# Expert loop: gate and up of an expert pair as one product of 512 columns in one PSUM bank

## The chip, the cores and the metric

The kernel runs on one core of a Trainium2 chip. The metric is the device time of one execution in microseconds (us). The kernel before took 1553.9 us (median of 3 runs, 1553.81 to 1555.06).

## What is computed

One step of a two-layer decoder over 264 tokens (256 of a prompt, 8 samples), all in fp32. Each layer has a mixer and then a mixture of experts; the change touches the experts alone. Of the reference, cut to that part:

```python
def moe(h, w_router, b_router, w_gate, w_up, w_down, ws_gate, ws_up, ws_down):
    x = h.reshape(-1, D)                                   # 264 tokens x 1024
    ...                                                    # sigmoid scores, best 4 of 8 groups, top 8 of 64 experts
    combine = ...                                          # (T, 64): a token's weight for an expert, or 0
    for gi in range(N_GROUPS):
        hg = jnp.einsum('td,edf->tef', x, w_gate[sl])      # 1024 -> 256 for each expert
        hu = jnp.einsum('td,edf->tef', x, w_up[sl])
        hw = jax.nn.silu(hg) * hu * combine[:, sl, None]
        routed = routed + jnp.einsum('tef,efd->td', hw, w_down[sl])
    shared = (jax.nn.silu(x @ ws_gate) * (x @ ws_up)) @ ws_down
    return (routed + shared).reshape(Bn, L, D)
```

## The kernel before

Engines and semaphores are programmed by hand: each engine has its own block with its instructions in order, and `wait_ge` on named semaphores ties them together. The order on an engine is the order in its block.

**Expert loop.** Experts go in pairs, 32 pairs a layer (`NPAIR`), two layers. Each pair has 128 slots of tokens, 64 for each of its two experts `e`. The loop body of `pe`, `act`, `dve` and `pool` is written out for four pairs (`EBODY`). A pair needs six weight blocks ("units") of 1 MiB: gate, up and down of two experts. They lie in a ring of 12 slots (`ring`, `ESLOTS`), so two pairs fit; SyncE (`expert_load`, line 516) refills a slot as soon as `unit_used` says that TensorE is through with it.

**TensorE for one pair, in order** (lines 1105 to 1156):
1. `product(0)`: gate. For each of 8 chunks `c` of the 1024 inputs and each `e`, a product of 256 columns; expert 0 writes partitions 0 to 63 and expert 1 partitions 64 to 127 of PSUM bank 0, columns 0 to 255. Stationary is the 128x64 block of tokens (`xgT`), moving are 256 columns of the ring.
2. `slots()`: three transposes that turn the slot choice of the pair after next into token rows (bank 4).
3. `product(1)`: up, the same into bank 1.
4. The combine: 8 products of 264 columns, one for each output chunk `c`, that spread the finished rows of the pair before (`gout_tiles`) back over the tokens. They use banks 5 to 7 in turn: chunk `c` waits until VectorE has added chunk `c - 3` to the sum (`cb_add`).
5. Two transposes of the hidden rows `ghid` (wait for `ghid` of this pair), into bank 0, columns 256 to 511.
6. `rows_in`: eight transposes of the next pair's gathered tokens.
7. The down product: 8 products of 512 columns into banks 2 and 3.

Every fp32 product is two LDWEIGHTS and two MATMUL instructions in the trace, every transpose one of each.

**ScalarE for one pair:** Silu of the gate (waits for two `unit_used`), copy of the turned slots (`slot_tokens`), copy of the turned hidden rows, two copies of turned tokens, one copy of half of the down result (`os_a`).

**VectorE for one pair** (lines 1903 to 1914): `choose` (L1868), `take_weights` (L1881, L1882), `take_slots` (L1873, L1876; waits for ScalarE's `slot_tokens`), then `ghid` = Silu x weight x up (L1910), then the eight additions `add_back` (L1887), then the copy of the other half of the down result (L1914).

**GpSimd** gathers the token rows of the pair after next by an indirect DMA (L654) as soon as `take_slots` has written their indices.

Of the kernel before, what the change touches and what calls it, by code (L numbers as in the profile page):

```python
# [17 lines left out]
ALU = mybir.AluOpType  # L18
ACT = mybir.ActivationFunctionType
AX = mybir.AxisListType  # L20

P = 128
# [39 lines left out]
EBODY = 4  # L62
NTURN = NPAIR // EBODY
PU = 6
RU = NPAIR * PU


SEL_R = NPAIR + 2
# [101 lines left out]
def build(nc, ins, outs):  # L170
# [12 lines left out]
    with ExitStack() as ctx:  # L183
# [275 lines left out]
        def eslot(j):  # L459

            return (j + PU) % ESLOTS
# [5 lines left out]
        def _(sp):  # L467
# [45 lines left out]

            def expert_load(l, pair2, j):

                sp.dma_start(ring[:, eslot(j), :], expert_src(l, pair2 + (j // PU * 2 + j % 2), j % PU // 2)).then_inc(eload[eslot(j)], 16)

            def experts(l, last):

                sp.wait_ge(S["htok_out"], 32 * (l + 1))  # L520
                for n, j in sorted((last - 1 - ((last - 1 - j) % MSLOTS), j) for j in range(MSLOTS)):
                    wait_used(n)
                    expert_load(l, 0, PU + j)
                sp.wait_ge(S["round_set"], l + 1)
                first = sp.value_load(nrounds[0:1, 0:1], min_val=1, max_val=MAXR) if l else 0
                end = sp.value_load(nrounds[0:1, l:l + 1], min_val=1, max_val=(l + 1) * MAXR)

                with sp.Fori(first, end) as r:
                    with sp.Fori(0, RU // ESLOTS - 1) as i:
                        for j in range(ESLOTS):  # L530
                            sp.wait_ge(S["unit_used"], r * RU + i * ESLOTS + (j + 1) + ONE)
                            expert_load(l, (i + 1) * 4, j)

                    with sp.If(r + 1 < end):
                        for j in range(ESLOTS):
                            sp.wait_ge(S["unit_used"], r * RU + (RU - ESLOTS) + (j + 1) + ONE)
                            expert_load(l, 0, j)

                if l == 0:
                    sp.wait_ge(S["unit_used"], end * RU + ONE)  # L540

# [149 lines left out]
        def _(pe):  # L691
# [330 lines left out]
            def moe(l):  # L1022
# [76 lines left out]
                with pe.Fori(first, end) as r:  # L1099
# [4 lines left out]
                    with pe.Fori(0, NTURN) as i:  # L1104
                        for b in range(EBODY):
                            done1 = r * NPAIR + i * EBODY + (b + 1)
                            nb = (b + 1) % 2
                            s0 = eslot((b % 2) * PU)

                            def arrived_units(kind):  # L1110
                                for e in range(2):
                                    pe.wait_ge(eload[s0 + 2 * kind + e], r * (RU // ESLOTS * 16) + i * 32 + 16 * (b // 2 + 1))

                            def product(kind):
                                arrived_units(kind)
                                for c in range(DT):
                                    for e in range(2):
                                        x = mm(psum[64 * e:64 * e + 64, kind, 0:DE], xgT[:, c, 64 * e:64 * e + 64],
                                               ring[:, s0 + 2 * kind + e, c * DE:(c + 1) * DE], c == 0, c == DT - 1)
                                        if c == DT - 1:  # L1120
                                            x.then_inc(S["unit_used"], 1)

                            pe.wait_ge(S["xt_sb"], r * XT_R + i * 8 + (2 * b + 2))
                            pe.wait_ge(S["gsil"], done1 - 1 + ONE)
                            product(0)

                            pe.wait_ge(S["sel"], r * SEL_R + i * EBODY + (b + 3))
                            slots()

                            pe.wait_ge(S["ghid"], done1 - 1 + ONE)  # L1130
                            product(1)

                            pe.wait_ge(S["os_a"], done1 - 1 + ONE)
                            pe.wait_ge(S["os_b"], done1 - 1 + ONE)
                            for c in range(DT):
                                pe.wait_ge(S["cb_add"], r * CB_R + i * 32 + (8 * b + max(c - 2, 0)) + BACK0)
                                mm(psum[:, back_bank(c), 0:T], gout_tiles[:, c], selT[(b + 3) % 4]).then_inc(S["cb_mm"], 1)

                            pe.wait_ge(S["ghid"], done1 + ONE)
                            for j in range(2):  # L1140
                                last = tr(psum[:, 0, (2 + j) * P:(3 + j) * P], ghid[:, j])
                            last.then_inc(S["ht_mm"], 1)

                            pe.wait_ge(S["gat_" + "ab"[nb]], r * GAT_R + i * 32 + 16 * ((b + 1) // 2 + 1))
                            pe.wait_ge(S["selT_sb"], r * SEL_R + i * EBODY + (b + 3))
                            rows_in(xg[nb], r * CB_R + i * 32 + (8 * b + 6) + BACK0)

                            pe.wait_ge(S["ht_sb"], done1 + ONE)
                            arrived_units(2)
                            for n in range(2):  # L1150
                                for j in range(2):
                                    for e in range(2):
                                        x = mm(psum[64 * e:64 * e + 64, 2 + n, :], ghT[:, j, 64 * e:64 * e + 64],
                                               ring[:, s0 + 4 + e, j * D + n * 512:j * D + n * 512 + 512], j == 0, j == 1)
                                        if n == 1 and j == 1:
                                            x.then_inc(S["unit_used"], 1)
# [105 lines left out]
        def _(act):  # L1262
# [111 lines left out]
            def moe(l):  # L1374
# [35 lines left out]
                with act.Fori(first, end) as r:  # L1410
                    act.wait_ge(S["unit_used"], r * RU + ONE)
                    rows_in(r * XT_R)
                    with act.Fori(0, NTURN) as i:
                        for b in range(EBODY):
                            done1 = r * NPAIR + i * EBODY + (b + 1)
                            used0 = r * RU + i * (EBODY * PU) + b * PU
# [5 lines left out]
                            act.wait_ge(S["ht_mm"], done1)  # L1422
                            act.wait_ge(S["unit_used"], used0 + 4 + ONE)
                            f(ghT, psum[:, 0, 2 * P:4 * P].rearrange("p (j s) -> p j s", j=2), ACT.Copy).then_inc(S["ht_sb"], 1)
                            rows_in(r * XT_R + i * 8 + (2 * b + 2))
                            act.wait_ge(S["unit_used"], used0 + 6 + ONE)
# [47 lines left out]
        def _(dve):  # L1474
# [331 lines left out]
            def moe(l):  # L1806
# [91 lines left out]
                with dve.Fori(first, end) as r:  # L1898
                    with dve.Fori(0, NTURN) as i:
                        for b in range(EBODY):  # L1900
                            done1 = r * NPAIR + i * EBODY + (b + 1)
                            used0 = r * RU + i * (EBODY * PU) + b * PU
                            choose(i * 8 + (2 * b + 4))
                            take_weights(b, i * 8 + 2 * b, r * XT_R + i * 8 + (2 * b + 2))
                            take_slots((b + 2) % 4, r * SEL_R + i * EBODY + (b + 3))

                            dve.wait_ge(S["gsil"], done1 + ONE)
                            dve.wait_ge(S["wt_set"], done1 + ONE)
                            dve.wait_ge(S["unit_used"], used0 + 4 + ONE)
                            V.scalar_tensor_tensor(ghid.rearrange("p j f -> p f j"), gsil.rearrange("p (f j) -> p f j", j=2), wt[:, b:b + 1], psum[:, 1, 0:DE].rearrange("p (f j) -> p f j", j=2), ALU.mult, ALU.mult).then_inc(S["ghid"], 1)  # L1910
                            dve.wait_ge(S["cb_add"], r * CB_R + i * 32 + 8 * b + BACK0)
                            add_back(r * CB_R + i * 32 + 8 * b)
                            dve.wait_ge(S["unit_used"], used0 + 6 + ONE)
# [91 lines left out]
```

## Time and profile before

| what | value |
|---|---|
| time, median of 3 runs | 1553.9 us |
| profiled execution: its span, first to last instruction | 1551.6 us |
| TensorE matmul (PE) busy | 1472.9 us, 95% |
| TensorE weight load (PEld) busy | 982.9 us, 63% |
| VectorE (DVE) busy | 626.2 us, 40% |
| ScalarE (ACT) busy | 299.1 us, 19% |
| DMA moved, over the span | 523.24 MB, mean 337 GB/s |
| TensorE's granted clock, mean | 0.974 of full |

The profile is of one execution. Busy shares are averages over stages with different limits; the two expert loops lie at about 328 to 835 us and 1018 to 1525 us. Matmuls are pipelined and their ends are modelled, so a busy PE is not PE at its peak. Where the timeline gives "x32" the row is a run of 32 instructions, its second number the time from the first's start to the last's end. What stands in brackets at a row's end is the engine's idle time before it and what ended it.

### The profile page before, as it was taken

How to read it: one execution, taken by the hardware profiler on the slowest of the kernel's cores; microseconds unless marked ns; L12 is line 12 of the kernel's file. 1: busy time of each engine (PE TensorE's matmuls, PEld its weight loads, DVE VectorE, ACT ScalarE, POOL GpSimd, SP SyncE). 2: the span in 40 equal slices, each digit the busy share in tenths (PEclk: the TensorE clock that was granted, in tenths of full speed). 3: DMA queues.
4: the chain of work that ended last, by engine and by line, in shares of the span. 5: the costliest groups of instructions: out<-in, count | busy, mean ns of one | idle time of the engine just before them, and what ended most of it. 6: DMA issues, size and time to landing. Idle time of an engine off the chain costs nothing. (4 is left out here: it accounts for less than half of the span.)

```text
span 1551.6 us, 29339 instructions
## 1 busy us (share of the span) xinstructions
PE 1472.9 (95%) x11071; PEld 982.9 (63%) x11071; DVE 626.2 (40%) x1628; ACT 299.1 (19%) x624; POOL 116.3 (7%) x122
## 2 busy tenths in 40 slices
PE   5999889989999999999998999799999999999996
PEld 2767777556666666666665688666666666666664
DVE  2038573723334343433335233733433334343434
ACT  0013112311111111111113221321111111111112
POOL 0000143000000000000000000100000000000000
PEclk8999798999999999999999999899999999999998
DMA  9996524779999999999993871389999999999971
GB/s 390 362 366 272 178 55 182 285 299 404 409 420 420 410 417 412 412 415 410 418 401 144 329 296 44 120 338 400 419 415 418 419 411 413 417 414 417 413 294 29
DMA packets 81361, 523.24 MB, mean 337 GB/s; under 512 B 14213, under 2 KB 14341, under 8 KB 21019
## 3 DMA queue, kind: packets, MB, share of 16 engines
q1 hardware_dynamic: 68587, 495.84, 78.6%
q0 software_dynamic: 12720, 26.63, 5.1%
q8 instruction: 40, 0.66, 0.2%
q14 instruction: 14, 0.11, 0.0%
HBM read 537.18 MB, written 4.74 MB: 349 GB/s over the span
## 5 line engine op out<-in xcount | busy, mean ns | idle before, releaser
L693 PE MATMUL psum<-ring,arena 128*64 128x256 f32 (+2 forms) x5552 | 706.7, 412 | 4.3 <-ACT arena L1264 2.3
L693 PEld LDWEIGHTS psum<-ring,arena 128*64 128x64 f32 (+1 forms) x5552 | 369.8, 139 | 297.8 <-issue 160.9
L1264 ACT ACTIVATE arena<-psum 128x256 f32<-128x256 f32 (+4 forms) x464 | 210.4, 489 | 1024.2 <-PE psum L693 529.0
L693 PE MATMUL psum<-arena 128*128 128x264 f32 (+2 forms) x1840 | 285.5, 324 | 4.1 <-DVE arena L1720 2.1
L693 PEld LDWEIGHTS psum<-arena 128*128 128x128 f32 (+1 forms) x1840 | 225.1, 171 | 62.7 <-issue 28.4
L1887 DVE TENSOR_TENSOR arena<-arena,psum 128x264 f32<-128x264 f32 x528 | 226.6, 429 | 9.3 <-PE psum L693 2.0
L693 PE MATMUL psum<-hT,ring 128*128 128x264 f32 x928 | 215.8, 390 | 6.2 <-DVE hT L1587 2.7
L693 PEld LDWEIGHTS psum<-hT,ring 128*128 128x128 f32 x928 | 176.4, 192 | 48.3 <-issue 19.9
L1914 DVE COPY arena<-psum 128x512 f32<-128x512 f32 x64 | 44.3, 692 | 274.1 <-PE psum L693 274.1
L654 POOL DMA_INDIRECT arena<-h_rows,slot_idx x68 | 67.6, 995 | 972.7 <-DVE slot_idx L1876 916.6
L696 PE MATMUL psum<-K,arena 128*128 128x128 f32 (+4 forms) x961 | 125.6, 270 | 7.3 <-DMA arena<-h_rows,slot_idx 5.4
L696 PEld LDWEIGHTS psum<-K,arena 128*128 128x128 f32 (+4 forms) x961 | 105.5, 139 | 42.2 <-issue 30.9
L1910 DVE SCALAR_TENSOR_TENSOR arena<-arena,psum 128x256 f32<-128x256 f32 x64 | 42.7, 667 | 163.9 <-PE psum L693 163.9
L1873 DVE CUSTOM_DVE_ANT_0 arena<-arena,K 128x264 f32<-128x264 f32 x68 | 29.4, 433 | 196.7 <-ACT arena L1264 196.7
L693 PE MATMUL psum<-arena,ring 64*64 64x64 f32 (+2 forms) x576 | 61.2, 293 | 10.4 <-issue 4.5
L693 PE MATMUL psum<-ring,cT 128*32 128x512 f32 x384 | 54.3, 683 | 14.8 <-DMA ring<-in_w_mod 14.8
L693 PEld LDWEIGHTS psum<-arena,ring 64*64 64x64 f32 (+1 forms) x576 | 52.1, 181 | 17.6 <-issue 8.3
L1868 DVE TENSOR_TENSOR arena<-K,arena 88x384 f32<-88x384 f32 x68 | 37.1, 545 | 10.7 <-ACT arena L1264 8.3
L693 PEld LDWEIGHTS psum<-ring,cT 128*32 128x32 f32 x384 | 10.9, 121 | 42.6 <-issue 30.6
L693 PE MATMUL psum<-arena,K 128*32 128x66 f32 (+2 forms) x348 | 27.6, 294 | 8.3 <-ACT arena L1264 8.2
L1264 ACT ACTIVATE ring<-psum 128x264 f32<-128x264 f32 (+3 forms) x24 | 13.2, 566 | 92.3 <-PE psum L693 80.8
L693 PEld LDWEIGHTS psum<-arena,K 128*32 128x32 f32 (+2 forms) x348 | 19.3, 141 | 17.1 <-ACT arena L1264 13.8
(210 smaller groups left out, 478.8 us busy)
## 6 DMA issues: line engine op xcount, KB each, us to landing
ring<-in_moe_w_gate SPq DMA_DIRECT2D x128, 1024.0 KB, 11.4
ring<-in_moe_w_up SPq DMA_DIRECT2D x128, 1024.0 KB, 12.6
ring<-in_moe_w_down SPq DMA_DIRECT2D x128, 1024.0 KB, 9.5
ring<-in_w_mod SPq DMA_DIRECT2D x48, 1024.0 KB, 9.0
ring<-in_ab_w_in SPq DMA_DIRECT2D x13, 1024.0 KB, 7.8
ring<-in_gm_w_in SPq DMA_DIRECT2D x8, 1024.0 KB, 8.6
ring<-in_ab_w_out SPq DMA_DIRECT2D x4, 1024.0 KB, 5.7
ring<-in_gm_w_out SPq DMA_DIRECT2D x4, 1024.0 KB, 6.9
```

The source lines that it names most:

```text
L654: pool.indirect_dma_start(xg[jj % 2], None, h_rows[l], bass.IndirectOffsetOnAxis(slot_idx[:, jj:jj + 1], 0), bounds_check=T - 1, oob_is_er ...
L693: return nc.tensor.matmul(out, lhsT, rhs, start=start, stop=stop)
L696: return nc.tensor.transpose(out, in_, ident[0:in_.shape[0], 0:in_.shape[0]])
L1264: return nc.scalar.activation(out, in_, func, **kw)
L1868: V.tensor_tensor(slotsel[0:TR], iota, over(p, CAP), ALU.is_equal).then_inc(S["sel"], 1)
L1873: V.tensor_tensor_reduce(sel_tok, selT[jj], K[:, C_IOTA:C_IOTA + T], 1.0, float(NO_ROW), ALU.mult, ALU.add, idxf[:, jj:jj + 1]).then_inc(S ...
L1887: V.tensor_tensor(yacc[:, c, :], yacc[:, c, :], psum[:, back_bank(c), 0:T], ALU.add).then_inc(S["cb_add"], 1)
L1910: V.scalar_tensor_tensor(ghid.rearrange("p j f -> p f j"), gsil.rearrange("p (f j) -> p f j", j=2), wt[:, b:b + 1], psum[:, 1, 0:DE].rearr ...
L1914: V.tensor_copy(gout_tiles[:, :, 64:128], psum[:, 3, :].rearrange("p (d c) -> p c d", c=DT)).then_inc(S["os_b"], 1)
```

## The change

Gate and up of an expert are one product: its moving operand is a pair of pieces of 256 columns from two neighbouring ring slots, its output the 512 columns of bank 0, gate in the first half and up in the second. `slots()` follows it. For this, the ring order of a pair's units becomes gate 0, up 0, gate 1, up 1, down 0, down 1 (`UNIT_OF`), `unit_used` counts four products of a pair instead of six (`USES`, `USED_AT`), and the hidden rows are turned into bank 1 instead of bank 0. SyncE, ScalarE and VectorE wait for other counts; the order of the work on ScalarE and VectorE is as before.

```diff
 PU = 6
-RU = NPAIR * PU
+UNIT_OF = ((0, 0), (0, 1), (1, 0), (1, 1), (0, 2), (1, 2))
+USED_AT = (1, 1, 2, 2, 3, 4)
+USES = 4
+RU = NPAIR * USES
...
-                            sp.wait_ge(S["unit_used"], r * RU + i * ESLOTS + (j + 1) + ONE)
+                            sp.wait_ge(S["unit_used"], r * RU + i * (2 * USES) + (j // PU * USES + USED_AT[j % PU]) + ONE)
                             expert_load(l, (i + 1) * 4, j)
...
                             pe.wait_ge(S["xt_sb"], r * XT_R + i * 8 + (2 * b + 2))
-                            pe.wait_ge(S["gsil"], done1 - 1 + ONE)
-                            product(0)
+                            pe.wait_ge(S["ghid"], done1 - 1 + ONE)
+                            for c in range(DT):
+                                for e in range(2):
+                                    if c == 0:
+                                        arrived_unit(2 * e)
+                                        arrived_unit(2 * e + 1)
+                                    x = mm(psum[64 * e:64 * e + 64, 0, :].rearrange("p (k f) -> p k f", k=2), xgT[:, c, 64 * e:64 * e + 64],
+                                           ring[:, s0 + 2 * e:s0 + 2 * e + 2, c * DE:(c + 1) * DE], c == 0, c == DT - 1)
+                                    if c == DT - 1:
+                                        x.then_inc(S["unit_used"], 1)
 
                             pe.wait_ge(S["sel"], r * SEL_R + i * EBODY + (b + 3))
                             slots()
 
-                            pe.wait_ge(S["ghid"], done1 - 1 + ONE)
-                            product(1)
-
                             pe.wait_ge(S["os_a"], done1 - 1 + ONE)
                             pe.wait_ge(S["os_b"], done1 - 1 + ONE)
                             for c in range(DT):
...
                             for j in range(2):
-                                last = tr(psum[:, 0, (2 + j) * P:(3 + j) * P], ghid[:, j])
+                                last = tr(psum[:, 1, j * P:(j + 1) * P], ghid[:, j])
...
                             dve.wait_ge(S["gsil"], done1 + ONE)
                             dve.wait_ge(S["wt_set"], done1 + ONE)
-                            dve.wait_ge(S["unit_used"], used0 + 4 + ONE)
-                            V.scalar_tensor_tensor(ghid..., psum[:, 1, 0:DE]..., ALU.mult, ALU.mult).then_inc(S["ghid"], 1)
+                            dve.wait_ge(S["unit_used"], used0 + 2 + ONE)
+                            V.scalar_tensor_tensor(ghid..., psum[:, 0, DE:2 * DE]..., ALU.mult, ALU.mult).then_inc(S["ghid"], 1)
                             dve.wait_ge(S["cb_add"], r * CB_R + i * 32 + 8 * b + BACK0)
                             add_back(r * CB_R + i * 32 + 8 * b)
```

## Rows read from the trace of the kernel before

**Rows 1.** Stretch of the loop: length; PE, PEld, DVE, ACT, POOL busy; PEclk, DMA share, GB/s.
```profile
400.00:500.00 100.00, 100.00 (x686) 63.09 (x682) 38.85 (x103) 16.24 (x36) 6.93 (x7) 1.00 1.01 418
```

**Rows 2.** Waits at 400 to 800 us: engine's, then SyncE's queue: us, times, longest.
```profile
DVE arena L1873 <- ACT arena L1264: 71.7, 25, 2.9
DVE arena L1910 <- PE psum L693: 66.6, 26, 2.6
...
SPq L516 <- PE psum L693: 319.4, 76, 7.5
```

**Rows 3.** Line 1914, 400 to 800 us: durations, first and last start.
```profile
L1914 DVE COPY arena<-psum x25: 690/692/692, 410.3 to 791.1; 128x512 f32<-128x512 f32 x25
```

**Rows 4.** Timeline of one pair, TensorE: start, us, instruction, count.
```profile
604.01 0.28 PEld L696 LDWEIGHTS psum<-K,arena 88*128 88x128 f32 x3 [0.39 <-issue]
604.39 3.67 PE L693 MATMUL psum<-ring,arena 128*64 128x256 f32 x32
608.00 3.41 PEld L693 LDWEIGHTS psum<-arena 128*128 128x128 f32 x16 [0.39 <-issue]
613.33 0.14 PEld L693 LDWEIGHTS psum<-ring,arena 128*64 128x64 f32 x2 [0.29 <-issue]
616.33 1.65 PEld L693 LDWEIGHTS psum<-ring,arena 128*64 128x64 f32 x16 [0.29 <-issue]
```

**Rows 5.** The same timeline, ScalarE and VectorE.
```profile
604.23 0.67 ACT L1264 ACTIVATE arena<-psum 128x256 f32<-128x256 f32 x2 [2.93 <-PE psum L693]
604.93 0.43 DVE L1873 CUSTOM_DVE_ANT_0 arena<-arena,K 128x264 f32<-128x264 f32 x1 [2.85 <-ACT arena L1264]
605.41 0.15 DVE L1876 CAST slot_idx<-arena 128x1 uint32<-128x1 f32 x1
606.41 0.99 POOL L654 DMA_INDIRECT arena<-h_rows,slot_idx  x1 [14.81 <-DVE slot_idx L1876]
608.14 0.67 DVE L1910 SCALAR_TENSOR_TENSOR arena<-arena,psum 128x256 f32<-128x256 f32 x1 [2.58 <-PE psum L693]
608.75 3.55 DVE L1887 TENSOR_TENSOR arena<-arena,psum 128x264 f32<-128x264 f32 x8
```

**Rows 6.** Timeline in short windows: weight loads and products of 256 columns, one by one.
```profile
604.45 0.14 PEld L693 LDWEIGHTS psum<-ring,arena 128*64 128x64 f32 x2
607.47 0.14 PEld L693 LDWEIGHTS psum<-ring,arena 128*64 128x64 f32 x2
607.68 0.39 PE L693 MATMUL psum<-ring,arena 128*64 128x256 f32 x2
```

**Rows 7.** The same, of the combine.
```profile
608.55 0.39 PE L693 MATMUL psum<-arena 128*128 128x264 f32 x1
609.44 0.39 PE L693 MATMUL psum<-arena 128*128 128x264 f32 x1
```

**Rows 8.** Timeline at the second loop's start.
```profile
1006.04 0.70 DVE L1893 TENSOR_TENSOR arena<-arena,psum 128x528 f32<-128x528 f32 x1 [1.47 <-PE psum L693]
1006.82 2.52 PEld L693 LDWEIGHTS psum<-arena,ring 128*128 128x128 f32 x12 [0.82 <-issue]
1007.13 0.15 DVE L1876 CAST slot_idx<-arena 128x1 uint32<-128x1 f32 x1
1007.21 0.55 DVE L1868 TENSOR_TENSOR arena<-K,arena 88x384 f32<-88x384 f32 x1
1018.00 3.67 PE L693 MATMUL psum<-ring,arena 128*64 128x256 f32 x32 [1.16 <-ACT arena L1264]
```

**Rows 9.** The page's DMA issues: count, KB each, us from issue to landing.
```profile
ring<-in_moe_w_up SPq DMA_DIRECT2D x128, 1024.0 KB, 12.6
```

**Rows 10.** A stretch that waits for weights, columns as in the first group.
```profile
10.00:20.00 10.00, 7.85 (x100) 2.67 (x96) 1.00 (x2) 0.32 (x1) 0.00 (x0) 1.00 1.01 424
```

**Rows 11.** Timeline at the first loop's start.
```profile
325.59 1.09 PE L696 MATMUL psum<-K,arena 128*128 128x128 f32 x8 [4.17 <-DMA arena<-h_rows,slot_idx]
327.84 6.46 PE L693 MATMUL psum<-ring,arena 128*64 128x256 f32 x32 [1.16 <-ACT arena L1264]
```

More of the change, by code:

```diff
@@ L514, in expert_load @@
             def expert_load(l, pair2, j):
-                sp.dma_start(ring[:, eslot(j), :], expert_src(l, pair2 + (j // PU * 2 + j % 2), j % PU // 2)).then_inc(eload[eslot(j)], 16)
+                sp.dma_start(ring[:, eslot(j), :], expert_src(l, pair2 + (j // PU * 2 + UNIT_OF[j % PU][0]), UNIT_OF[j % PU][1])).then_inc(eload[eslot(j)], 16)
             def experts(l, last):
@@ L528, in experts @@
                 with sp.Fori(first, end) as r:
-                    with sp.Fori(0, RU // ESLOTS - 1) as i:
+                    with sp.Fori(0, NPAIR * PU // ESLOTS - 1) as i:
                         for j in range(ESLOTS):
-                            sp.wait_ge(S["unit_used"], r * RU + i * ESLOTS + (j + 1) + ONE)
+                            sp.wait_ge(S["unit_used"], r * RU + i * (2 * USES) + (j // PU * USES + USED_AT[j % PU]) + ONE)
                             expert_load(l, (i + 1) * 4, j)
@@ L535, in experts @@
                         for j in range(ESLOTS):
-                            sp.wait_ge(S["unit_used"], r * RU + (RU - ESLOTS) + (j + 1) + ONE)
+                            sp.wait_ge(S["unit_used"], r * RU + (RU - 2 * USES) + (j // PU * USES + USED_AT[j % PU]) + ONE)
                             expert_load(l, 0, j)
@@ L1108, in moe, with arrived_unit @@
                             s0 = eslot((b % 2) * PU)
-                            def arrived_units(kind):
-                                for e in range(2):
[L1112 to L1123, printed above, removed]
-                            pe.wait_ge(S["gsil"], done1 - 1 + ONE)
-                            product(0)
+                            def arrived_unit(u):
+                                pe.wait_ge(eload[s0 + u], r * (NPAIR * PU // ESLOTS * 16) + i * 32 + 16 * (b // 2 + 1))
+                            pe.wait_ge(S["xt_sb"], r * XT_R + i * 8 + (2 * b + 2))
+                            pe.wait_ge(S["ghid"], done1 - 1 + ONE)
+                            for c in range(DT):
+                                for e in range(2):
+                                    if c == 0:
[5 more added lines that the diff above has]
+                                        x.then_inc(S["unit_used"], 1)
                             pe.wait_ge(S["sel"], r * SEL_R + i * EBODY + (b + 3))
                             slots()
-                            pe.wait_ge(S["ghid"], done1 - 1 + ONE)
-                            product(1)
                             pe.wait_ge(S["os_a"], done1 - 1 + ONE)
@@ L1148, in moe @@
                             pe.wait_ge(S["ht_sb"], done1 + ONE)
-                            arrived_units(2)
+                            arrived_unit(4)
+                            arrived_unit(5)
                             for n in range(2):
@@ L1415, in moe @@
                             done1 = r * NPAIR + i * EBODY + (b + 1)
-                            used0 = r * RU + i * (EBODY * PU) + b * PU
+                            used0 = r * RU + i * (EBODY * USES) + b * USES
                             act.wait_ge(S["unit_used"], used0 + 2 + ONE)
@@ L1422, in moe @@
                             act.wait_ge(S["ht_mm"], done1)
+                            act.wait_ge(S["unit_used"], used0 + 2 + ONE)
+                            f(ghT, psum[:, 1, 0:2 * P].rearrange("p (j s) -> p j s", j=2), ACT.Copy).then_inc(S["ht_sb"], 1)
+                            rows_in(r * XT_R + i * 8 + (2 * b + 2))
                             act.wait_ge(S["unit_used"], used0 + 4 + ONE)
-                            f(ghT, psum[:, 0, 2 * P:4 * P].rearrange("p (j s) -> p j s", j=2), ACT.Copy).then_inc(S["ht_sb"], 1)
-                            rows_in(r * XT_R + i * 8 + (2 * b + 2))
-                            act.wait_ge(S["unit_used"], used0 + 6 + ONE)
                             f(gout_tiles[:, :, 0:64], psum[:, 2, :].rearrange("p (d c) -> p c d", c=DT), ACT.Copy).then_inc(S["os_a"], 1)
@@ L1901, in moe @@
                             done1 = r * NPAIR + i * EBODY + (b + 1)
-                            used0 = r * RU + i * (EBODY * PU) + b * PU
+                            used0 = r * RU + i * (EBODY * USES) + b * USES
                             choose(i * 8 + (2 * b + 4))
@@ L1908, in moe @@
                             dve.wait_ge(S["wt_set"], done1 + ONE)
-                            dve.wait_ge(S["unit_used"], used0 + 4 + ONE)
-                            V.scalar_tensor_tensor(ghid.rearrange("p j f -> p f j"), gsil.rearrange("p (f j) -> p f j", j=2), wt[:, b:b + 1], psum[:, 1, 0:DE].rearrange("p (f j) -> p f j", j=2), ALU.mult, ALU.mult).then_inc(S["ghid"], 1)
+                            dve.wait_ge(S["unit_used"], used0 + 2 + ONE)
+                            V.scalar_tensor_tensor(ghid.rearrange("p j f -> p f j"), gsil.rearrange("p (f j) -> p f j", j=2), wt[:, b:b + 1], psum[:, 0, DE:2 * DE].rearrange("p (f j) -> p f j", j=2), ALU.mult, ALU.mult).then_inc(S["ghid"], 1)
                             dve.wait_ge(S["cb_add"], r * CB_R + i * 32 + 8 * b + BACK0)
                             add_back(r * CB_R + i * 32 + 8 * b)
-                            dve.wait_ge(S["unit_used"], used0 + 6 + ONE)
+                            dve.wait_ge(S["unit_used"], used0 + 4 + ONE)
                             V.tensor_copy(gout_tiles[:, :, 64:128], psum[:, 3, :].rearrange("p (d c) -> p c d", c=DT)).then_inc(S["os_b"], 1)
```

## The prediction

> **What bounds the kernel now.** I read the stretches by engine first, then the waits, then one pair on the timeline. In an expert loop TensorE is busy without a break at the full granted clock, while the DMA engines are busy too (share 1.01, 418 GB/s) [rows 1]. The waits say which of the two leads: between 400 and 800 us no row has TensorE's matmuls waiting for a DMA or for an engine; VectorE waits for TensorE and for ScalarE, and the load queue of SyncE waits 319.4 us for TensorE to free ring slots [rows 2]. So TensorE sets the pace, and the weights arrive early. Line 1914 runs once a pair: 25 starts from 410.3 to 791.1 us are 24 periods of 15.87 us [rows 3]. With 32 pairs in each of two layers that is 64 x 15.87 = 1016 of the 1551.6 us. A change of 0.1 us a pair is worth 6.4 us.
>
> On the timeline of one pair [rows 4] the first product of a pair starts at S = 616.33 - 15.87 = 600.46. Then come the slots' transposes at 604.01, the up product at 604.39, the combine's first weight load at 608.00, later the down product, and the next pair at 616.33. Beside it, ScalarE and VectorE [rows 5] do Silu and slot copy (604.23), the slot indices (604.93 to 605.56), then VectorE idles 2.58 us until the up product ends, multiplies `ghid` at 608.14 and adds from 608.75. The point to see: the chain Silu, slot copy, indices runs **under the up product** now, and so costs nothing.
>
> **The change part by part.**
>
> *Columns.* Two products of 256 columns become one of 512. A step here is one pass of both experts side by side. Fourteen steps of 256 lie between the weight loads at 604.45 and 607.47: 0.2157 us each [rows 6]. Seven steps of 512 in the down product lie between 613.33 and 616.33: 0.4286 us each [rows 4]. So 32 x 0.2157 = 6.90 us become 16 x 0.4286 = 6.86 us: 0.05 us less. That the moving operand lies in two pieces has no row; at worst a break costs what starting another 256-column product costs (the same 0.003 us a step, 0.05 us in all), at best nothing. I take nothing.
>
> *Edges.* The last 256-column step starts at 607.68 [rows 6], so it is through at 607.90, but the combine's first load starts at 608.00 [rows 4]: 0.10 us lost where 64-column weights give way to 128-column ones. The same 0.10 lies ahead of the slots' transposes (604.01 - 600.46 - 16 x 0.2157). The combine's later products start 0.222 us apart (608.55 to 609.44 is four starts) [rows 7], so its first was at 608.11, 7.65 us after S. After the change there are 6.86 us of product, one edge of 0.10, the three transposes (their loads take 0.28 [rows 4], I take 0.30) and then the combine without an edge: 7.26 us. Saved: 0.39 us a pair, 0.05 by columns and 0.34 by edges. If the edges stayed, it would be 0.05.
>
> The Trainium skill, "TensorEngine Tiling (Array Packing)", section "Key Properties", has a rule for these edges: a change of tiling mode drains TensorE. By it two of three such changes go and the 0.34 us is real; without it the saving would be the 0.05 us of the columns. The 0.10 us gaps are what this trace shows of it.
>
> *The chain that loses its cover.* The slots' transposes and the combine now follow the product directly, with nothing between. Let t be the start of the slots' first load: before 604.01, after S + 6.86 + 0.10 = S + 6.96. From rows 5: ScalarE starts at t + 0.22, VectorE's L1873 at t + 0.92 and the index cast at t + 1.40. `ghid` stands next in VectorE's queue and no longer has to wait for an up product; the instruction after a cast starts 0.08 us after it (1007.13, 1007.21) [rows 8]: t + 1.48. The first addition starts 0.61 us after `ghid` (608.14, 608.75) and eight take 3.55, so 0.44 each [rows 5]: it ends at t + 2.53. From VectorE's end to TensorE's weight load are 0.08 us (1006.04 + 0.70 to 1006.82) [rows 8], and another 0.10 to the product, as at 608.00: t + 2.71.
>
> Who waits for that: chunk 3 of the combine takes the bank of chunk 0 and waits for that first addition. It would start at S + 7.26 + 6 x 0.222 = S + 8.59. It can start at S + 6.96 + 2.71 = S + 9.67. So a **new wait of 1.08 us** stands in every pair, with all of TensorE's later work queued behind it. Before, chunk 3 started at 609.44 = S + 8.98 [rows 7], with the first addition over at 609.19, just in time. The pair becomes 9.67 - 8.98 = 0.69 us longer. Behind it both engines go on at 0.44 us a chunk, and where an addition is due at the same time as its product I allow 0.03: **0.72 us a pair**.
>
> Bounds: 0.50 if the restart's 0.10 is hidden and the additions run somewhat faster than 0.44 when they follow without waiting; 0.98 if VectorE's three waits ahead of `ghid`, which show no price in the trace, cost 0.1 and the restart 0.2. The rows lie nearer the lower half of this, hence 0.72.
>
> The Trainium skill, "VectorE: DVE Perf Modes", section "The DRAIN you can't avoid", says that the next operation does not start until the pipe is empty. By it `ghid` would follow the cast after its 0.15 and the addition after the 0.67 of `ghid`: 0.13 us more a pair, 8 us in all. Here an addition starts at 608.75, before 608.14 + 0.67 = 608.81 [rows 5]; the trace disagrees, and the sum goes without it.
>
> *Loads.* SyncE now issues four loads together at the product's end and two at the down product's. Nothing else waits on its queue. A gate slot was free at t = S + 3.55 and needed two periods after S, 28.2 us later; now it is free at S + 6.9 and needed 2 x 16.6 - 6.9 = 26.3 us later. Median landing is 12.6 us [rows 9]; even six loads in a row, 6.29 MB at the 424 GB/s that the stage waiting for weights reached [rows 10], take 14.8. Covered. The gather (GpSimd) goes out 1.0 us after the cast starts [rows 5] and now stands behind the four loads: up to 9.9 us more. It is needed for the next pair's token transposes, over 18 us later. Covered too. The new counts of `unit_used`, the bank of the hidden transposes and the order of units in the ring cost nothing: they change numbers, not instructions.
>
> *Sum.* 64 x 0.72 = 46 us. 1551.6 + 46 = 1598; the median lies 2.3 us above the span, so **1600 us**.
>
> **The rivals.**
> 1. *Edges stay* (0.05 saved, not 0.39): +0.34 a pair, 1.06 in all, 64 x 1.06 = 68: 1622 us. For it: no row shows transposes followed by a combine. Against: the 0.10 us gap appears at both ends of the 64-column work.
> 2. *No new wait; faster.* Place: chunk 3's wait. It decides when the first addition ends by t + 1.45 instead of t + 2.53, by the chain not running as long as in rows 5. Then 0.39 us is gained a pair, 64 x 0.39 = 25; the DMA allows less: a period moves 418 x 15.87 = 6.63 MB [rows 1], which at 424 GB/s [rows 10] takes 15.64 us, a gain of 0.23 a pair: 1539 us. Against: VectorE's order is fixed, and each link stands in rows 5.
> 3. *Both cancel.* A chain 0.7 us shorter than I add up would leave the time at 1554 us.
> 4. *The clock falls* in each new gap. At the first loop's start TensorE waited 4.17 us, and then 32 products took 6.46 us where they take 3.67 at full clock [rows 11, 4]: about 2.8 us lost. Every pair so would be +180 us: about 1780. Against: at the second loop's start a wait of 1.16 us, longer than the new one, was followed by 3.67 us for the same 32 [rows 8].
> 5. *The change doesn't do what it says*: the 512-column products of the two experts don't run side by side, each pair +6.86 us: about 2040. Against: the down product has the same shape and does [rows 4].
>
> **How the numbers follow.** Forecast 78%; edges stay 10%; no wait 5%; both cancel 2%; clock 3%; not side by side 2%. The bounds 0.50 and 0.98 a pair give 1586 and 1617; with the first rival the range goes from 1586 to 1622, and holds the forecast and that rival but for a tenth of their tails. A measurement of this kernel can tell about 0.2% (3 us) from no change. Slower: 78 + 10 + 3 + 2 = 93%; faster 5%; the same 2%.
>
> **What would show it.** Line 1914's period near 16.6 us. In each pair a gap of about 1 us on TensorE inside the combine, ahead of chunk 3, with VectorE's L1887 as its cause. VectorE's wait ahead of `ghid` (2.58 us) gone, and the eight additions no longer beside the first chunks. The product's 16 steps at 0.43 us; the slots' transposes and the combine without an edge between them. DMA share below 1.01. I'd be wrong if TensorE shows no wait in the combine, if it waits for weights instead, or if the granted clock in the loops is below 1.00.

## The result and the profile after

The changed kernel takes 1603.2 us (median of 4 runs, 1601.9 to 1604.9) against 1554.5 us for the kernel before on the same chip: ratio 1.0315, 95% interval 1.0297 to 1.0333. It is 3% slower. The profiled execution has a span of 1599.8 us, 48.2 us more than before.

First the page's own line on busy time. TensorE issues fewer instructions (9023 matmuls instead of 11071) and is busy 9 us less; it is not the work that grew.

```profile
PE 1463.9 (92%) x9023; PEld 834.3 (52%) x9023; DVE 607.1 (38%) x1628; ACT 300.7 (19%) x624; POOL 116.0 (7%) x122
```

Two stretches of the loop (columns as in [rows 1]), then the waits between 400 and 800 us (engine's, then SyncE's queue; compare [rows 2]):

```profile
400.00:500.00 100.00, 94.70 (x464) 45.60 (x462) 34.18 (x96) 16.39 (x36) 5.93 (x6) 1.00 0.99 397
700.00:800.00 100.00, 94.94 (x466) 45.75 (x464) 34.17 (x96) 16.39 (x36) 5.93 (x6) 1.00 0.99 394
```
```profile
PEld psum L696 <- DVE arena L1886: 30.7, 24, 1.5
PE psum L696 <- DVE arena L1886: 20.7, 24, 1.0
...
DVE arena L1909 <- issue: 1.6, 6, 0.3
...
SPq L519 <- PE psum L696: 316.0, 48, 7.6
```

TensorE now idles 5% of the loop at full clock, and a row stands there that the kernel before didn't have: its weight loads wait for line 1886, VectorE's additions, once in each of 24 pairs, 1.28 us each time. The row of VectorE waiting for the up product ahead of the hidden product (2.58 us a pair in [rows 2, 5]) is gone. TensorE still waits for no load.

One pair of the changed kernel on the timeline (lines of the listing have moved by a few: 1872, 1875, 1909, 1886 and 1913 are what were 1873, 1876, 1910, 1887 and 1914):

```profile
380.66 7.04 PE L696 MATMUL psum<-ring,arena 128*64 128x512 f32 x32
...
380.90 0.69 DVE L1913 COPY arena<-psum 128x512 f32<-128x512 f32 x1 [4.28 <-PE psum L696]
...
387.62 0.28 PEld L699 LDWEIGHTS psum<-K,arena 88*128 88x128 f32 x3 [0.81 <-issue]
...
387.83 1.19 PEld L696 LDWEIGHTS psum<-arena 128*128 128x128 f32 x6
387.84 0.67 ACT L1263 ACTIVATE arena<-psum 128x256 f32<-128x256 f32 x2 [6.35 <-PE psum L696]
...
388.54 0.43 DVE L1872 CUSTOM_DVE_ANT_0 arena<-arena,K 128x264 f32<-128x264 f32 x1 [6.27 <-ACT arena L1263]
...
389.02 0.15 DVE L1875 CAST slot_idx<-arena 128x1 uint32<-128x1 f32 x1
389.27 0.66 DVE L1909 SCALAR_TENSOR_TENSOR arena<-arena,psum 128x256 f32<-128x256 f32 x1
389.77 3.43 DVE L1886 TENSOR_TENSOR arena<-arena,psum 128x264 f32<-128x264 f32 x8
...
390.24 2.08 PEld L696 LDWEIGHTS psum<-arena 128*128 128x128 f32 x10 [1.22 <-DVE arena L1886]
...
392.35 1.24 PEld L699 LDWEIGHTS psum<-K,arena 128*128 128x128 f32 x10
...
397.49 0.69 DVE L1913 COPY arena<-psum 128x512 f32<-128x512 f32 x1 [4.28 <-PE psum L696]
...
404.21 0.28 PEld L699 LDWEIGHTS psum<-K,arena 88*128 88x128 f32 x3 [0.81 <-issue]
...
404.50 0.67 ACT L1263 ACTIVATE arena<-psum 128x256 f32<-128x256 f32 x2 [6.42 <-PE psum L696]
...
405.68 0.15 DVE L1875 CAST slot_idx<-arena 128x1 uint32<-128x1 f32 x1
406.10 0.66 DVE L1909 SCALAR_TENSOR_TENSOR arena<-arena,psum 128x256 f32<-128x256 f32 x1 [0.27 <-issue]
...
414.31 0.69 DVE L1913 COPY arena<-psum 128x512 f32<-128x512 f32 x1 [4.28 <-PE psum L696]
```

The combine's loads come in two groups: six for chunks 0 to 2 (387.83), then a gap, then ten for chunks 3 to 7 (390.24). From the slots' transposes to the end of the gap, ScalarE and VectorE work through Silu, slot copy, indices, hidden product and first addition, one behind the other. In [rows 4] the combine's sixteen loads stand in one row. From one copy of line 1913 to the next are 16.59 us (380.90 to 397.49); every fourth pair, at the turn of the written-out loop, takes 16.82 (397.49 to 414.31). The mean over 23 periods is 16.64 us against 15.87 in [rows 3]:

```profile
L1913 DVE COPY arena<-psum x24: 691/693/693, 414.3 to 797.0; 128x512 f32<-128x512 f32 x24
```

That accounts for the whole: 64 x (16.64 - 15.87) = 49 us, of the 48.2 us that the span grew.

### The profile page after: what moved, and what is told of

Read it like the earlier page. It is cut to its first block and busy times, and to the rows that moved or that the text cites. A ratio compares the mean times of both kernels' runs of the same rounds, so it can differ in the third digit from the quotient of the medians.

```text
span 1599.8 us, 25123 instructions
## 1 busy us (share of the span) xinstructions
PE 1463.9 (92%) x9023; PEld 834.3 (52%) x9023; DVE 607.1 (38%) x1628; ACT 300.7 (19%) x624; POOL 116.0 (7%) x122
## 5 line engine op out<-in xcount | busy, mean ns | idle before, releaser
L696 PE MATMUL psum<-ring,arena 128*64 128x512 f32 (+1 forms) x3504 | 688.9, 553 | 4.2 <-ACT arena L1263 2.3
L696 PEld LDWEIGHTS psum<-ring,arena 128*64 128x64 f32 (+1 forms) x3504 | 230.2, 140 | 414.9 <-issue 412.8
L696 PE MATMUL psum<-arena 128*128 128x264 f32 (+2 forms) x1840 | 298.4, 326 | 59.3 <-DVE arena L1886 55.3
L696 PEld LDWEIGHTS psum<-arena 128*128 128x128 f32 (+1 forms) x1840 | 221.1, 171 | 114.8 <-DVE arena L1886 81.8
L1886 DVE TENSOR_TENSOR arena<-arena,psum 128x264 f32<-128x264 f32 x528 | 214.1, 426 | 14.7 <-PE psum L696 2.0
```

Source lines behind the costliest of these rows:

```text
L696: return nc.tensor.matmul(out, lhsT, rhs, start=start, stop=stop)
L1886: V.tensor_tensor(yacc[:, c, :], yacc[:, c, :], psum[:, back_bank(c), 0:T], ALU.add).then_inc(S["cb_add"], 1)
```

## The experiments

Theory *order*: moving the slots' transposes behind the product takes the cover off the chain slots, slot copy, indices, hidden product, first addition, and chunk 3 of the combine waits for its end; it also saves two changes between 64-column and 128-column weights. Rival *shape*: the 512-column product with its operand in two pieces costs more than it looks. Rival *ring*: four loads at once and slots freed later cost time. "Pair" below is the time from one copy of half the down result on VectorE to the next, in an ordinary pair and at the turn of the loop. Each ratio is to the kernel before on the chip of that run, hence the range in the first row.

| kernel | us | ratio to before, 95% | pair, turn (us) |
|---|---|---|---|
| before | 1551.9 to 1554.5 | 1 | 15.87, 15.87 |
| changed | 1603.2 | 1.0315 (1.0297 to 1.0333) | 16.59, 16.82 |
| two products, slots late | 1602.9 | 1.0316 (1.0293 to 1.0338) | 16.62, 16.78 |
| changed, one piece | 1602.2 | 1.0317 (1.0295 to 1.0340) | 16.59, 16.82 |
| changed, one more instruction ahead | 1620.0 | 1.0419 (1.0404 to 1.0434) | 16.87, 17.02 |
| changed, slots inside the product | 1574.6 | 1.0136 (1.0121 to 1.0150) | 16.20, 16.34 |
| changed, five banks | 1547.6 | 0.9966 (0.9954 to 0.9977) | 15.71, 15.94 |
| two products, slots late, five banks | 1549.2 | 0.9957 (0.9941 to 0.9972) | 15.74, 15.91 |
| changed, indices last | 1542.7 | 0.9939 (0.9923 to 0.9955) | 15.67, 15.84 |
| changed, six banks | 1534.7 | 0.9881 (0.9861 to 0.9900) | 15.52, 15.52, late pairs more |
| changed, six banks, indices last | 1533.4 | 0.9871 (0.9852 to 0.9889) | 15.52, 15.52, late pairs more |
| before, five banks | 1554.3 | 0.9999 (0.9985 to 1.0012) | 15.87, 15.87 |

### Two products, slots late

```diff
                             pe.wait_ge(S["gsil"], done1 - 1 + ONE)
                             product(0)
-                            pe.wait_ge(S["sel"], r * SEL_R + i * EBODY + (b + 3))
-                            slots()
                             pe.wait_ge(S["ghid"], done1 - 1 + ONE)
                             product(1)
+                            pe.wait_ge(S["sel"], r * SEL_R + i * EBODY + (b + 3))
+                            slots()
```

> The kernel before with one edit: the slots' transposes stand behind the up product instead of between gate and up. Gate and up stay two products of 256 columns, the ring order is the old one. Theory 'order' (the time comes from the chain slots, slot copy, indices, hidden product, first addition, which has lost the up product as its cover): the combine's chunk 3 waits as in the changed kernel, the pair is about 16.65 us, the time about 1605 us (1598 to 1612), some 2 us of it because the columns' saving is missing. Rival 'shape' (the 512-column product with its operand in two pieces costs more than it looks) and rival 'ring' (four loads at once, slots freed later): neither is in this kernel, so 1554 us or, with fewer edges, down to about 1535.

1602.9 us, the changed kernel's time to within the interval. Its waits between 400 and 800 us have the same new rows:

```profile
PEld psum L693 <- DVE arena L1887: 30.0, 24, 1.4
PE psum L693 <- DVE arena L1887: 20.0, 24, 1.0
```

So the place of the slots alone makes the loss. The 512-column product, the two-piece operand and the new ring order are not in this kernel.

### Six banks

```diff
+        def loop_bank(c):
+            return (6, 7, 1, 5, 2, 3, 6, 7)[c]
...
                             for c in range(DT):
-                                pe.wait_ge(S["cb_add"], r * CB_R + i * 32 + (8 * b + max(c - 2, 0)) + BACK0)
-                                mm(psum[:, back_bank(c), 0:T], ...)
+                                pe.wait_ge(S["cb_add"], r * CB_R + i * 32 + (8 * b + max(c - 5, 0)) + BACK0)
+                                mm(psum[:, loop_bank(c), 0:T], ...)
...
                             pe.wait_ge(S["ghid"], done1 + ONE)
+                            pe.wait_ge(S["cb_add"], r * CB_R + i * 32 + (8 * b + 3) + BACK0)
...
-                            rows_in(xg[nb], r * CB_R + i * 32 + (8 * b + 6) + BACK0)
+                            rows_in(xg[nb], r * CB_R + i * 32 + (8 * b + 4) + BACK0)
 
                             pe.wait_ge(S["ht_sb"], done1 + ONE)
+                            pe.wait_ge(S["cb_add"], r * CB_R + i * 32 + (8 * b + 6) + BACK0)
...
-                            add_back(r * CB_R + i * 32 + 8 * b)
+                            add_back(r * CB_R + i * 32 + 8 * b, loop_bank)
```

> The changed kernel, but the combine's eight chunks go over six PSUM banks (6, 7, 1, 5, 2, 3, 6, 7) instead of three, so that chunk 3 waits for no addition of its own pair; chunks 6 and 7 wait for additions 0 and 1, and the later users of banks 1, 5, 2 and 3 wait for theirs. Nothing else moves. Theory 'order': the wait of about 1 us inside the combine is gone and what the change saves shows: 15.87 - 0.33 = 15.54 us a pair by TensorE (the changed kernel's product and edges give 7.32 us to the combine's first product, 7.65 before), 1533 us; the weights may then bound it (about 15.5 to 15.6 us a pair at 424 GB/s): 1530 to 1545. Rivals 'shape' and 'ring': the time stays within 10 us of 1603, since neither is touched.

1534.7 us, 1.2% faster than before. The combine's loads run in one row again, beside the same chain (timeline of one pair):

```profile
612.57 0.28 PEld L703 LDWEIGHTS psum<-K,arena 88*128 88x128 f32 x3 [0.81 <-issue]
612.78 3.42 PEld L700 LDWEIGHTS psum<-arena 128*128 128x128 f32 x16
...
614.22 0.66 DVE L1915 SCALAR_TENSOR_TENSOR arena<-arena,psum 128x256 f32<-128x256 f32 x1
...
614.73 2.79 DVE L1892 TENSOR_TENSOR arena<-arena,psum 128x264 f32<-128x264 f32 x8
```

The additions are as late as in the changed kernel (2.16 us after the slots' first load), but nothing of their own pair waits for the first one. The pair is 15.52 us: without the wait, the changed order saves 0.35 us a pair against the kernel before (which was run with five banks, below, and gained nothing by them, but not with six). The wait itself is worth 16.59 - 15.52 = 1.07 us.

### Indices last

```diff
-                            take_slots((b + 2) % 4, r * SEL_R + i * EBODY + (b + 3))
                             dve.wait_ge(S["gsil"], done1 + ONE)
...
                             add_back(r * CB_R + i * 32 + 8 * b)
+                            take_slots((b + 2) % 4, r * SEL_R + i * EBODY + (b + 3))
```

> The changed kernel, but VectorE makes the slot indices behind the eight additions instead of ahead of the hidden product. The gather goes out about 4 us later in its pair. Theory 'order': the chain ahead of the first addition shrinks to Silu, hidden product, addition: the addition ends 1.57 us after the slots' first load instead of 2.58, chunk 3 waits about 0.1 us, the pair is about 15.63 us and the time about 1539 us (1533 to 1548). If the later gather comes too late for the next pair's token transposes, TensorE waits there and it is above 1554. Rivals 'shape' and 'ring': about 1600.

1542.7 us. The chain is shorter by the slot copy and the indices, and the wait of TensorE shrinks to 0.31 us of idle weight loads (timeline of one pair):

```profile
618.71 0.28 PEld L699 LDWEIGHTS psum<-K,arena 88*128 88x128 f32 x3 [0.81 <-issue]
...
619.44 0.67 DVE L1908 SCALAR_TENSOR_TENSOR arena<-arena,psum 128x256 f32<-128x256 f32 x1 [6.07 <-ACT arena L1263]
619.95 3.44 DVE L1886 TENSOR_TENSOR arena<-arena,psum 128x264 f32<-128x264 f32 x8
...
620.42 2.08 PEld L696 LDWEIGHTS psum<-arena 128*128 128x128 f32 x10 [0.31 <-DVE arena L1886]
```

Chunk 3 starts loading 1.71 us after the slots' first load instead of 2.62. The gather, now 3.7 us later in its pair, makes nobody wait. Moving one call in VectorE's program turns the changed kernel from 3% slower to 0.6% faster.

### One piece

```diff
-    x = mm(psum[64 * e:64 * e + 64, 0, :].rearrange("p (k f) -> p k f", k=2), xgT[:, c, 64 * e:64 * e + 64],
-           ring[:, s0 + 2 * e:s0 + 2 * e + 2, c * DE:(c + 1) * DE], c == 0, c == DT - 1)
+    x = mm(psum[64 * e:64 * e + 64, 0, :], xgT[:, c, 64 * e:64 * e + 64],
+           ring[:, s0 + 2 * e + c // 4, (c % 4) * 512:(c % 4) * 512 + 512], c == 0, c == DT - 1)
```

> The changed kernel, but the moving operand of each 512-column product is one piece of 512 columns of a ring slot instead of two pieces of 256 from two slots. It reads the same slots at the same times; the columns then belong to other chunks, so gate and up are not the reference's. Theory 'order': as the changed kernel, 1603 us within 3. Rival 'shape': if the two pieces cost, the 16 steps fall below 0.4286 us each or the edge behind them shortens, and the time falls by up to the whole 49 us.

1602.2 us and the same 16.59 us a pair. Two pieces of the moving operand cost nothing here.

### Slots inside the product

```diff
                             for c in range(DT):
+                                if c == DT // 2:
+                                    pe.wait_ge(S["sel"], r * SEL_R + i * EBODY + (b + 3))
+                                    slots()
                                 for e in range(2):
...
-                            pe.wait_ge(S["sel"], r * SEL_R + i * EBODY + (b + 3))
-                            slots()
...
+                            act.wait_ge(S["slot_tr"], r * SEL_R + i * EBODY + (b + 3))
+                            slot_tokens((b + 2) % 4)
                             act.wait_ge(S["unit_used"], used0 + 2 + ONE)
```

> The changed kernel, but the slots' transposes stand in the middle of the 512-column product (after 4 of its 8 chunks) and ScalarE copies the slots ahead of Silu, so that slot copy and indices run under the product again. Theory 'order' with the term 'edges': the chain behind the product is that of the run with the indices last (chunk 3's product 1.8 us after the combine's first load), but leaving and re-entering 64-column weights costs again what the kernel before paid, so the combine's first load comes about 7.45 us after the pair's start: the pair is 15.87 + 0.3 = 16.15 us, 1570 us (1560 to 1580). If the edges cost nothing and only 256 against 512 columns does, the transposes cost their 0.3 us wherever they stand: about 1543. Rivals 'shape' and 'ring': about 1600.

1574.6 us, near the 1570 of theory *order* with its edges and far from the 1543 without them. Against the run with the indices last, whose chain behind the product is the same (chunk 3's load 1.71 us after the first 128-wide load in both), the pair is 16.20 - 15.67 = 0.53 us longer. With the indices last the slots' transposes run beside that chain, here ahead of it, so that their 0.21 us (387.62 to 387.83 above) come onto the path. The rest, 0.32 us, is what it costs to leave the 64-column weights and come back to them. The timeline shows it by itself:

```profile
622.47 0.69 DVE L1913 COPY arena<-psum 128x512 f32<-128x512 f32 x1 [4.28 <-PE psum L696]
...
629.72 1.19 PEld L696 LDWEIGHTS psum<-arena 128*128 128x128 f32 x6 [0.81 <-issue]
...
631.43 2.08 PEld L696 LDWEIGHTS psum<-arena 128*128 128x128 f32 x10 [0.52 <-DVE arena L1886]
```

From the copy to the combine's first load are 7.25 us (622.47 to 629.72), in the changed kernel 6.93 (380.90 to 387.83): the same product and the same three transposes lie between, and 0.32 us more.

### One more instruction ahead

```diff
+                            dve.wait_ge(S["idx"], r * SEL_R + i * EBODY + (b + 3))
+                            V.tensor_tensor(sel_tok, selT[(b + 2) % 4], K[:, C_IOTA:C_IOTA + T], ALU.mult)
                             dve.wait_ge(S["gsil"], done1 + ONE)
```

> The changed kernel with one more VectorE instruction between the slot indices and the hidden product (a product of 264 columns into the scratch of the slot indices, which nothing reads). Theory 'order': everything that VectorE does there stands on the path one for one: 0.36 to 0.50 us a pair more, 64 x that: 1603 + 23 to 32 = 1626 to 1635 us. Rivals 'shape' and 'ring': VectorE is busy 38% of the time and not on the path, no change, 1603.

1620.0 us: longer, but by 0.28 us a pair, less than the 0.36 expected at least. The timeline shows why:

```profile
626.14 0.28 PEld L699 LDWEIGHTS psum<-K,arena 88*128 88x128 f32 x3 [0.81 <-issue]
...
627.54 0.15 DVE L1875 CAST slot_idx<-arena 128x1 uint32<-128x1 f32 x1
627.73 0.43 DVE L1907 TENSOR_TENSOR arena<-arena,K 128x264 f32<-128x264 f32 x1
628.08 0.65 DVE L1911 SCALAR_TENSOR_TENSOR arena<-arena,psum 128x256 f32<-128x256 f32 x1
...
629.04 2.08 PEld L696 LDWEIGHTS psum<-arena 128*128 128x128 f32 x10 [1.50 <-DVE arena L1886]
```

The hidden product starts 1.94 us after the slots' first load instead of 1.65, so the added instruction moves it by 0.29 us only: part of it ran in the 0.25 us that lay between cast and hidden product anyway. From there it is one for one: chunk 3's load moves from 2.62 to 2.90 us, the pair by 0.28. VectorE is busy 38% of the time, and what it does between product and first addition is on the path all the same.

### Five banks, before and after

```diff
+        def loop_bank(c):
+            return (5, 6, 7, 2, 3, 5, 6, 7)[c]
...
-                                pe.wait_ge(S["cb_add"], r * CB_R + i * 32 + (8 * b + max(c - 2, 0)) + BACK0)
+                                pe.wait_ge(S["cb_add"], r * CB_R + i * 32 + (8 * b + max(c - 4, 0)) + BACK0)
```

The same edit in the kernel before, in the changed kernel, and in the one with two products and late slots.

> The kernel before, but the combine's chunks go over five PSUM banks (5, 6, 7, 2, 3, 5, 6, 7) instead of three, and chunk 5 is the first that waits for an addition of its own pair. A control: in the kernel before the first addition is over before chunk 3 is due, so more banks take away no wait. Theory 'order': 1552 to 1554 us, as before within 3. If more banks by themselves make the combine faster (a wait in it that the trace doesn't show), it falls by 10 us or more, and the run with six banks then shows less than it seems.

> The kernel before with the slots' transposes behind the up product (as in the first run) and the five banks of the control. Two products of 256 columns, the old ring order. It asks what of the saving is the 512 columns and what is the place of the slots. Theory 'order': the wait moves from chunk 3 to chunk 5 and shrinks from about 1.1 to about 0.2 us, the edges are saved as in the changed kernel: about 15.75 to 15.8 us a pair, 1546 to 1549 us, without any 512-column product. If the saving needs the 512 columns, it stays at 1555 to 1575.

> The changed kernel with the five banks of the control. Against the run with two products, late slots and the same five banks it differs by the 512-column product and the ring order alone. By steps of 0.4286 us for 512 and 0.2157 us for 256 columns the 512 columns are worth 16 x 0.003 = 0.05 us a pair, 3 us in all: 1546 us (1543 to 1550), beside 1549 there. If the 512 columns are worth more than that where no wait hides them, the gap is 8 us or more; if the four loads at once cost something, it is slower than that run.

The control stays where it was (1554.3 us, ratio 0.9999): in the kernel before, the banks were no limit. In both others the first wait moves from chunk 3 to chunk 5 and the time falls below before. The two differ by 0.03 us in an ordinary pair (15.71, 15.74) and by nothing that the times can tell (1547.6 and 1549.2 us): the 512-column product is worth about what its steps say, and the saving comes from where the slots stand. Three, five and six banks give a series: pairs of 16.59, 15.71 and 15.52 us.

### Six banks and indices last

The six banks' edit and the move of `take_slots` together.

> The changed kernel with both cures: six banks and the slot indices behind the additions. With six banks alone one wait is left, about 0.17 us ahead of the down product for addition 5, and the weights land about 17 us after issue instead of 9 to 11. With the indices last the additions end about 1 us earlier and that wait goes: 15.45 to 15.5 us a pair by TensorE, 1528 to 1531 us. Rival 'weights': the DMA engines are at their limit at 420 GB/s, so the pair can't get below about 15.55 us; then TensorE waits for loads in places and the time stays at 1533 to 1536.

1533.4 us, no better than six banks alone. Two things were wrong in what theory *order* expected. The 0.17 us ahead of the down product is no wait for an addition: it is there in every version, this one too, and belongs to the step from transposes to 64-column weights. And the rival *weights* was right. Line 1919 runs once a pair; between 1039.5 and 1349.8 us twenty periods are 15.52 us each, and so are the two up to 1380.85; then they are 16.1, 16.3, 15.9 and so on:

```profile
L1919 DVE COPY arena<-psum x21: 691/692/693, 1039.5 to 1349.8; 128x512 f32<-128x512 f32 x21
```
```profile
1380.85 0.69 DVE L1919 COPY arena<-psum 128x512 f32<-128x512 f32 x1 [3.74 <-PE psum L700]
...
1396.99 0.69 DVE L1919 COPY arena<-psum 128x512 f32<-128x512 f32 x1 [3.75 <-PE psum L700]
...
1413.25 0.69 DVE L1919 COPY arena<-psum 128x512 f32<-128x512 f32 x1 [3.74 <-PE psum L700]
```

The loads of gate and up take longer from issue to landing as the loop goes on (medians, 1030 to 1150 us, then 1300 to 1400 us):

```profile
ring<-in_moe_w_gate SPq DMA_DIRECT2D x16, 1024.0 KB, 11.7
ring<-in_moe_w_up SPq DMA_DIRECT2D x16, 1024.0 KB, 14.7
```
```profile
ring<-in_moe_w_gate SPq DMA_DIRECT2D x12, 1024.0 KB, 18.5
ring<-in_moe_w_up SPq DMA_DIRECT2D x12, 1024.0 KB, 20.5
```

In the first two long pairs the break stands at the start of the product. The trace gives it to "issue", not to a DMA, but the landing of the load that arrives last, the up block of the second expert, shows what it is. For each of the two pairs: the issue of that load, its time to landing, and the product's weight loads behind the break.

```profile
1358.48 0.37 SPq L523 DMA_DIRECT2D ring<-in_moe_w_up  x1
ring<-in_moe_w_up SPq DMA_DIRECT2D x1, 1024.0 KB, 22.6
1381.18 1.29 PEld L700 LDWEIGHTS psum<-ring,arena 128*64 128x64 f32 x8 [0.43 <-issue]
...
1373.82 0.38 SPq L523 DMA_DIRECT2D ring<-in_moe_w_up  x1
ring<-in_moe_w_up SPq DMA_DIRECT2D x1, 1024.0 KB, 23.5
1397.44 0.30 PEld L700 LDWEIGHTS psum<-ring,arena 128*64 128x64 f32 x4 [0.56 <-issue]
```

The first lands at 1358.48 + 22.6 = 1381.1 us, the second at 1373.82 + 23.5 = 1397.3, and the product goes on 0.1 us later each time: TensorE waits for weights. The DMA engines are busy all the time, at 420 GB/s (columns as in [rows 1]), and that isn't enough for 15.52 us a pair. By the 6.63 MB a pair that the prediction takes from [rows 1] it would be 15.8 us, an estimate. So the ring's lead is used up bit by bit, and from then on the loads set the pace.

```profile
1040.00:1300.00 260.00, 260.00 (x1293) 129.26 (x1291) 93.90 (x272) 45.67 (x102) 15.82 (x16) 1.00 1.01 420
```

## Why the prediction was right

**Bound, by period.** TensorE set the pace before, with no wait in the loop; the control with five banks bears it out. The whole loss lies in the 64 pairs.

**The chain.** This was the step on which the sign hung, and it held in place and in size. The slots' first load comes 6.96 us after the pair's start, as predicted (380.66 to 387.62). Chunk 3's load comes 2.62 us after that, predicted 2.61. The wait is 1.07 us by the six-bank run, predicted 1.08. That the total of the chain came out to the hundredth is luck; it hides errors of both signs. The hidden product starts 0.25 us behind the cast, not 0.08 (three waits stand ahead of it, each long satisfied; that they are the reason is inferred). The first addition starts 0.50 us behind the hidden product, not 0.61 as in [rows 5]. And from its start to chunk 3's load are 0.47 us (389.77 to 390.24), not 0.52. In the kernel before, the combine's first load starts only 0.14 us ahead of the hidden product, so that addition was waiting for its chunk of the combine; that the 0.61 was no price of VectorE's is inferred from this and from the 0.50 here, where the chunk is there early. The price of the three waits that the upper bound allowed for (0.1) thus came, at 0.17. That bound's two terms give 0.72 + 0.1 + 0.1 = 0.92 with a restart of 0.2 in place of 0.10, not the 0.98 stated; nothing hangs on it.

The rule of the Trainium skill that the prediction left aside ("VectorE: DVE Perf Modes", section "The DRAIN you can't avoid", by which the next operation waits for an empty pipe) does not describe this chain: additions start 0.50 us into a hidden product of 0.66, and 2.79 us for eight additions of some 0.43 us in the six-bank run means starts 0.34 us apart. The section itself adds that an operation that is not held starts earlier. The overlaps agree with that; no run here tests what holds one.

**Columns and edges.** Predicted 0.39 us a pair, 0.05 of columns and 0.34 of edges; the six-bank run shows 15.87 - 15.52 = 0.35. Columns are about 0.03 (the two kernels with five banks), edges 0.32 (slots inside the product). The drain at a change of tiling mode, which the Trainium skill states ("TensorEngine Tiling (Array Packing)", section "Key Properties"), fits this; its size is this kernel's, some 0.3 us for leaving and coming back.

**Loads.** Covered, as predicted: no load makes TensorE wait at 16.6 us a pair, and the gather does not, even 3.7 us later in the run with the indices last.

**The sum.** Predicted 0.72 us a pair; an ordinary pair shows 16.59 - 15.87 = 0.72. The second decimal is luck here too: 1.07 of wait less 0.35 saved, where the prediction had 1.08 less 0.39 and 0.03 allowed on top. What the sum lacked is the turn of the loop: 0.23 us at each of the seven turns inside each layer's loop, 14 x 0.23 = 3.2 us in all. In the kernel before it is hidden (15.87 in every pair). On the uncovered chain Silu of such a pair starts 0.29 us behind the slots' first load (404.21 to 404.50) instead of 0.22, and the hidden product 0.42 us behind its cast (405.68 to 406.10) instead of 0.25; both lengthen the wait. 1600 + 3.2 is the 1603 measured.

**The rivals.** "Edges stay" fell with the run that has the slots inside the product. "No new wait" was the right mechanism for another kernel: with the wait taken away the time is 1534.7 us, where that rival said 1539, held up by the weights as it said, though only late in each loop. "Both cancel", the clock (1.00 in both stretches above) and "not side by side" show nowhere.

## What to carry to other kernels

An instruction between two long ones on the busiest engine can be what gives a chain on other engines its cover: before moving it, write down what starts at its end and what must be over when the second long one ends. Few PSUM banks turn a consumer's delay at once into a wait of the producer; here three more banks, free at that time, took the whole wait away, and so nearly did moving work that nobody waits for behind work that somebody does. And a gap between two starts read in a kernel where the second waits for something else is no price of the engine.

## What the hardware showed that was not expected

- Satisfied waits ahead of a VectorE instruction seem not to be free: the next instruction starts 0.25 us behind the cast with three of them, 0.08 us without one [rows 8]. Behind the added instruction of 0.43 us, with the same three waits ahead of it, the hidden product starts 0.35 us later (627.73 to 628.08), about as additions follow each other, so a price shows only behind the short cast. At the turn of the written-out loop the pair is 0.14 to 0.24 us longer wherever this chain is not covered.
- Additions of 264 columns from PSUM, 0.43 us each, start 0.34 us apart when none of them waits.
- At 420 GB/s the median time to landing grows from 11.7 to 18.5 us (gate) and from 14.7 to 20.5 us (up) within one loop, and 22 pairs run at 15.52 us before TensorE is held up for the first time: the first two thirds of each loop do not tell whether the loads keep up.
